# A fused three-layer kernel: MLP openings with products side by side, earlier first scores, a later output split, two banks for half blocks

## The reference

```python
# layer 0: banded attention (16 heads of 64, 4 KV heads, band of 3 blocks of 128 keys, sinks) + memory attention
# layer 1: two RG-LRU scans (forward, backward) with conv and gate + memory attention
for l in range(2):
    h = rms_norm(x, mix_norm[l])
    mixed, mq = attn_mixer(h, ...) if l == 0 else lru_mixer(h, ...)
    mo = memory_attention(mq, mk, mv)            # 4 heads of 128, 256 memory keys
    x = x + concatenate([mixed, mo]) @ w_out[l]
    x = x + square(relu(rms_norm(x, mlp_norm[l]) @ w_up[l])) @ w_down[l]   # 4096 hidden
x = rms_norm(x, final_norm)
# layer 2: stick-breaking attention + sliding window with sinks, gated; modulation from c_2 @ w_ada_2
```

## Time and profile before

| what | value |
|---|---|
| median of 3 runs | 3047.69 us (3042.49 to 3051.21) |
| the profiled execution | 3045.61 us, its span 3043.8 us |
| PE / DVE / ACT / POOL busy | 97% / 70% / 41% / 3% of the span |
| granted TensorE clock, mean | 0.992 |
| DMA | 190 MB, 63 GB/s over the span |
| chain that ended last | PE 80%, DVE 10%, ACT 7%, issue 2% |

### The profile page before, as it was taken

One profiled execution on the slowest core, in us unless ns is written; L12 is line 12 of the kernel. 1 busy time (PEld: TensorE's weight loads), 2 busy tenths in 40 slices (PEclk: granted clock), 3 DMA queues, 4 the chain that ended last, 5 costly groups with the idle time before them and its releaser, 6 DMA issues.

```text
span 3043.8 us, 35198 instructions
## 1 busy us (share of the span) xinstructions
PE 2956.6 (97%) x13896; PEld 2311.9 (76%) x13896; DVE 2142.7 (70%) x3303; ACT 1243.6 (41%) x2121; POOL 89.9 (3%) x70
## 2 busy tenths in 40 slices
PE   8999989999999999999999999999999999999998
PEld 7885557878888888888877788888888786666666
DVE  7746866687777777689964887777777735566675
ACT  4214642432222222478832522222223516876652
POOL 0003520000000000000000000000000000000000
PEclk9999999999999999999999999999999999999999
DMA  4430024111111111211131011111111131000213
GB/s 155 118 94 8 1 98 140 55 50 51 52 56 49 49 56 56 101 45 46 52 139 42 21 56 56 53 46 56 56 50 61 49 126 34 21 21 22 97 52 114
DMA packets 72804, 190.47 MB, mean 63 GB/s; under 512 B 8320, under 2 KB 8704, under 8 KB 72512
## 3 DMA queue, kind: packets, MB, share of 16 engines
q1 hardware_dynamic: 72640, 188.23, 19.2%
HBM read 172.20 MB, written 14.68 MB: 61 GB/s over the span
## 4 chain that ended last, share of the span: by engine, by line
PE 80%; DVE 10%; ACT 7%; issue 2%; DMA 0%; POOL 0%; SPq 0%; DVEq 0%; ACTq 0%; POOLq 0%
PE PS L1490 42%; PE PS L279 25%; PE PS L366 2%; DVE sm L908 2%; PE PS L320 1%; ACT p L926 1%; PE PS L887 1%; PE PS L873 1%; PE PS L2784 1%; PE PS L2801 1%; PE PS L899 1%; PE PS L2775 1%; PE PS L1092 1%; PE PS L1084 1%; ACT p L233 1%
## 5 line engine op out<-in xcount | busy, mean ns | idle before, releaser
L1490 PE MATMUL PS<-p 128*128 128x512 f32 x5760 | 1318.0, 391 | 13.3 <-DVE p L1401 7.7
L1490 PEld LDWEIGHTS PS<-p 128*128 128x128 f32 x5760 | 1083.0, 188 | 246.6 <-ACT p L1395 8.5
L279 PE MATMUL PS<-p 128*128 128x512 f32 (+1 forms) x4560 | 1057.0, 390 | 26.3 <-DVE p L475 9.6
L279 PEld LDWEIGHTS PS<-p 128*128 128x128 f32 x4560 | 840.5, 189 | 231.5 <-issue 39.8
L1687 DVE TENSOR_TENSOR p<-p,PS 128x512 f32<-128x512 f32 x480 | 327.7, 683 | 64.5 <-PE PS L1490 51.2
L241 DVE TENSOR_TENSOR p<-p 128x1024 fp32r<-128x1024 f32 x138 | 163.7, 1190 | 142.5 <-ACT p L233 142.3
L1299 DVE TENSOR_TENSOR p<-p 128x512 fp32r<-128x512 f32 x224 | 154.2, 688 | 112.3 <-ACT p L1293 111.4
L1627 ACT ACTIVATE p<-p 128x512 fp32r<-128x512 f32 x128 | 80.2, 628 | 346.0 <-DVE p L1676 329.6
L1293 ACT ACTIVATE p<-p 128x512 fp32r<-128x512 f32 x224 | 140.1, 625 | 184.9 <-PE PS L1490 159.5
L233 ACT ACTIVATE p<-p 128x1024 fp32r<-128x1024 f32 x138 | 141.7, 1030 | 172.9 <-PE PS L279 111.5
L926 ACT ACTIVATE p<-PS,sm 128x256 f32<-128x256 f32 (+2 forms) x256 | 127.9, 508 | 173.7 <-DVE sm L914 94.1
(11 more groups left out here) (236 smaller groups left out, 2785.3 us busy)
## 6 DMA issues: line engine op xcount, KB each, us to landing
p<-in_in_dram SPq DMA_DIRECT2D x72, 512.0 KB, 3.5
p<-in_up_dram SPq DMA_DIRECT2D x128, 256.0 KB, 2.6
p<-in_dn_dram SPq DMA_DIRECT2D x128, 256.0 KB, 2.6
p<-in_out_dram SPq DMA_DIRECT2D x42, 512.0 KB, 3.6
p<-in_ada_dram SPq DMA_DIRECT2D x24, 512.0 KB, 3.6
p<-in_x_dram SPq DMA_DIRECT2D x16, 512.0 KB, 8.0
p<-in_kv_dram SPq DMA_DIRECT2D x16, 512.0 KB, 3.5
spill_dram<-p SPq DMA_DIRECT2D x16, 512.0 KB, 3.9
```

Of the source, the lines that this page charges most:

```text
L279: ins = e.matmul(ps[:, c:c + m], weights(b, j, wi), x[:, c:c + m], start=first and i == 0, stop=end and i == 2)
L1490: ins = e.matmul(PS[:, bank, :], w[:, wi, :], x[:, xi, :], start=start and i == 0, stop=stop and i == 2, skip_group_check=open_)
```

## The change

1. **First scores.** The score halves 0 and 1 of the banded attention are issued after mq0 2, ahead of mq0 3. DVE scales mq0 3 (`dve_last_queries`) between the stats of halves 1 and 2, ACT's exponentials of unit 1 wait for that. `END0` is gone.
2. **Output split behind the copies.** ACT's L1018 comes after its copies L952; DVE's L1047 (`out_low`) moves into the next unit, between the stats and the normalisation of j=0.
3. **Boundary to memory attention 0.** Memory scores 0 and 1 are issued in units 32 and 33 of the banded loop, before its last transposes and values; DVE and ACT do their stats and exponentials of unit 0 there. PE, DVE no longer wait for `END1`, ACT waits for the last values only; SP's loads of X still wait for `END1`.
4. **Half blocks in two banks.** Fills 0 and 2 use bank 6, the others bank 7, in both memory stages. In memory attention 0 the fills of units 7 and 8 move between values and transposes, that of unit 9 ahead of the values. The modulation products follow the first tile of the projection, in bank 6.
5. **Memory attention 1.** ACT and DVE do `y_half(0)` before the block split; DVE scales the queries before the block split.
6. **MLP openings (both).** PE does product 0, then k = 0 to 2 of products 1, 2, 3, then their k = 3, then the total, then products 4, 5, (1,0), 6, (1,1) to (1,5). Products (1,0) and (1,3) use bank 5, which the first down product also uses; it now waits for ("t11", l, 1). Ring part 3 moves ahead of the last inputs; ring 7 goes before 6; 9 to 12, S4 and the root's halves are interleaved anew, the root and `dve_t("11")` of pair 0 come later, `dve_t("11")` of pair 1 before the first addition.

```diff
@@ pe_values0
-            pe_project(P, e, "in0", 4, 8, Hk("x0"), ("mq0",), lambda n: [("mq0t", n)])
+            P.pair = 1
+            pe_project(P, e, "in0", 3, 8, Hk("x0"), ("mq0",), lambda n: [("mq0t", n)])
+            for hs in range(2):
+                n, kp, half, kbs = UNITS0[0]
+                pe_window_scores(P, e, "b0", hs, hs, score_view(hs, 128 * len(kbs), True), n, kp, half, kbs, Qt, Kt, 4, bias0,
+                                 [*(("rotated", x) for x in range(10)), P.held[2 * hs], P.held[2 * hs + 1], ("cb",)])
+            P.pair = 2
+            pe_project(P, e, "in0", 1, 8, Hk("x0"), ("mq0", 3), lambda n: [("mq0t", 3)])
@@ dve_banded0
+                    if hs == 2:
+                        dve_last_queries(V, e)
...
+                    if j == 0 and u >= 3 and UNITS0[u - 3][2] == 1:
+                        out_low(u - 3)
                     if 1 <= hs <= 64:
...
@@ pe_banded0
+                    if j == 0 and u >= 32:
+                        for b in range(2):
+                            P.held[2 * (u - 32) + b] = [("exp", "b0", 30 + u)]
+                        pe_mem_scores(P, e, "m0", u - 32, MQ, MK, [("mq0t", 3), *(("mk0", n) for n in range(4))])
@@ pe_mem0
-                if FILLS[u] > 1:
+                if FILLS[u] > 1 or u == 9:
                     fill()
                 if u >= 2:
                     pe_mem_values(P, e, "m0", u - 2, MV, PTM0, None)
+                if u in (7, 8):
+                    fill()
...
-            pe_mod(P, e)
             P.pair = 0
-            pe_project(P, e, "out0", 8, 4, MOk(MO0, "m0"), ("xo", 0), lambda n: [("xb", 0, n)])
+            pe_project(P, e, "out0", 8, 4, MOk(MO0, "m0"), ("xo", 0), lambda n: [("xb", 0, n)], first=lambda: pe_mod(P, e))
@@
+        def fill_bank(i):
+            return 6 if i in (0, 2) else 7
+        def bank_of(j, o):
+            return 5 if j == 1 and o in (0, 3) else BANK[o]
@@ pe_mlp
-            for o in range(3):
-                pe_product(P, e, l, 0, o)
+            pe_product(P, e, l, 0, 0)
+            for o in (1, 2, 3):
+                pe_product(P, e, l, 0, o, 0, 3)
+            for o in (1, 2, 3):
+                pe_product(P, e, l, 0, o, 3, 4)
             pe_total(P, e, ("x", l), SQX[0], SQX[1][7], X_SUMMED[l], p=3, more=SQX[1][6])
-            for o in range(3, 7):
-                pe_product(P, e, l, 0, o)
-            for o in range(6):
-                pe_product(P, e, l, 1, o)
+            for j, o in ((0, 4), (0, 5), (1, 0), (0, 6), (1, 1), (1, 2), (1, 3), (1, 4), (1, 5)):
+                pe_product(P, e, l, j, o)
+            P.held[5] = [("t11", l, 1)]
@@ dve_first_pairs
+            dve_s3(V, e, l, 0)
+            ring(7)
             ring(6)
-            dve_s3(V, e, l, 0)
             dve_t(V, e, l, 0, "21")
-            ring(7)
             dve_t(V, e, l, 0, "22")
-            dve_root(V, e, ("x", l), *ROOTX)
-            dve_t(V, e, l, 0, "11")
             ring(8)
...
             ring(13)
+            dve_t(V, e, l, 1, "11")
             add(0, 0)
-            dve_t(V, e, l, 1, "11")
@@ act_mem1, dve_mem1
+                if u == 0:
+                    y_half(0)
                 if u < 2:
                     fill()
-                if u == 0:
-                    y_half(0)
```

More of the change, by code:

```diff
@@ L839, in dve_values0 @@
             e.tensor_scalar(vec[:, NV0:NV0 + 24], C("sinks", 0, 24), -1.0, None, ALU.mult).then_inc(*V.did(("nsinks",)))
-            for n in range(4):
+            for n in range(3):
                 block_lo(V, e)
@@ L844, in dve_values0, with dve_last_queries @@
                 e.tensor_tensor(MQ[:, n, :], got(("mq0", n)), R0, ALU.mult).then_inc(*V.did(("mq0t", n)))
-        END0 = [("mq0", 3), ("whi", 33), ("mq0t", 3), ("clear",)]
+            block_lo(V, e)
+        def dve_last_queries(V, e):
+            for s in V.need(("mq0", 3, 0)):
+                e.wait_ge(*s)
+            e.tensor_tensor(MQ[:, 3, :], got(("mq0", 3, 0)), R0, ALU.mult).then_inc(*V.did(("mq0t", 3)))
         def score_view(hs, nk, full):
@@ L1021, in act_banded0, with out_low @@
                             act_copy(A, e, "b0", u - 1, kb, PT0, TB0, pt_free[kb])
+                    if j == 1 and u >= 2 and UNITS0[u - 2][2] == 1:
+                        src, hh, hl = out0_of(u - 2)
+                        for s in A.need(("pv", "b0", u - 2)):
+                            e.wait_ge(*s)
+                        e.activation(hh, src, ACT.Copy).then_inc(*A.did(("oh", "b0", u - 2)))
         def dve_banded0(V, e):
-            for s in V.need(*END0):
-                e.wait_ge(*s)
             pt_free = [None] * 3
+            def out_low(u):
+                src, hh, hl = out0_of(u)
+                for s in V.need(("oh", "b0", u)):
+                    e.wait_ge(*s)
+                e.tensor_tensor(hl, src, fz(hh), ALU.subtract).then_inc(*V.did(("ol", "b0", u)))
             for u in range(34):
@@ L1132, in pe_mem0 @@
         def pe_mem0(P, e):
-            for s in P.need(*END1):
-                e.wait_ge(*s)
             fills = [(n, hf) for n in range(8) for hf in range(2)]
@@ L1186, in dve_mem0 @@
         def dve_mem0(V, e):
-            for s in V.need(*END1):
-                e.wait_ge(*s)
             dve_cond(V, e)
@@ L1212, in dve_mem0 @@
                     dve_ada(V, e, 3 * u - 2)
-                fill()
+                if u < 7:
+                    fill()
                 if 1 <= u <= 8:
@@ L1609, in act_first_sum @@
                 e.wait_ge(*s)
-            e.activation(quota(j, "12"), PS[:, 0, :], ACT.Copy).then_inc(*A.did(("s1", l, j)))
+            e.activation(quota(j, "12"), PS[:, bank_of(j, 0), :], ACT.Copy).then_inc(*A.did(("s1", l, j)))
         SPOT = {"11": (0, 0), "21": (0, 1), "12": (1, 0), "22": (1, 1)}
@@ L1776, in dve_first_pairs @@
                 dve_made(V, e, l, 1, name)
+            dve_root(V, e, ("x", l), *ROOTX, only=0)
+            ring(9)
+            dve_root(V, e, ("x", l), *ROOTX, only=1)
+            ring(10)
+            dve_made(V, e, l, 1, "S4")
+            ring(11)
+            dve_t(V, e, l, 0, "11")
             dve_q(V, e, l, 0, "11")
             dve_r(V, e, l, 0, "21")
-            ring(9)
             dve_t(V, e, l, 0, "12")
@@ L1789, in dve_first_pairs @@
             dve_r(V, e, l, 0, "12")
-            ring(11)
             dve_down(V, e, l, 0, 1)
```

127 lines of the change are left out of this document (63 added, 64 removed).

## The result

| | before | after |
|---|---|---|
| median | 3048.03 us (4 runs, 3042.49 to 3051.21) | 3016.39 us (4 runs, 3014.92 to 3021.25) |
| ratio after/before, 95% interval | | 0.990, 0.9884 to 0.9917 |
| profiled execution, its span | 3045.6, 3043.8 us | 3016.5, 3014.7 us |
| granted TensorE clock, mean | 0.992 | 0.994 |

The change takes 31.6 us off the median and 29.1 us off the profiled span: 1%, and the interval leaves out 1. 3021 had been predicted, in 3008 to 3034.

The account below looks back on a forecast made before the run. PE, busy 2956.6 of 3043.8 us, was taken as the bound, leaving only its idle and low-clock time to win. Gains 5.8 + 3.7 + 3.5 + 2.4 + 9.2 + 1.8 = 26.4 us off 3047.7 gave 3021, range 3008 to 3034.

Parts of the forecast that it names:

- three small waits: Banded attention start: PE waits 0.3 us for bank 4, 0.9 for the normalisation, 0.4 for the copy out of bank 4.
- The first rival: Start of the banded attention stays at the lower clock: 5.8 us gain becomes 2.5, 3024.6 us; chance 0.15.
- The pair: Two banded units, one with an output: 11.66 us before, forecast to gain 0.31 us.
- number of places: Banded attention, output split: 0.31 us gained per pair of units, counted over 12 pairs, 3.7 us.
- what comes back: Banded pairs: 0.57 of the 0.88 us saved was to return as a wait on POOL's later scaling.
- The waits: Memory attention 0: second fill's 0.83 us and normalisation waits of 0.47 and 1.52 us shrink; gain 0.8 + 1.6.
- The modulation products cost the same where they stand now: Memory attention 0, first projection tile: moving these products was to bring no gain, nothing counted.
- The new wait: MLP openings, before the first down product: PE waits 5.7 and 6.4 us for bank 5, the kernel's longest.
- bank 5 is free in time: Rival, MLP openings: part of DVE's chain overlaps, up to 16.9 us more gain, 3004 us; chance 0.08.
- bank 5 comes later still: Rival, MLP openings: DVE waits for an unseen ACT copy or DMA, some 4 us each, 3030 us; chance 0.10.

Follow-up runs that it names:

- e6: Changed kernel with no scores ahead of the last query block, the banded attention starting as in the kernel before: 3021.12 us.
- e1: Changed kernel with the output split ahead of the copies again on ACT and DVE: 3016.99 us.
- e7: Changed kernel with DVE's low half of the output behind the normalisation again: 3017.4 us.
- e5: Changed kernel with DVE's evacuation of t11 of pair 1 moved up to behind the first down split: 3005.62 us.
- e2: Changed kernel with both MLP openings as they were before the change: 3022.23 us.
- e3: Changed kernel with memory attention 1's half blocks in bank 7 alone, the changed order kept: 3022.97 us.
- e4: Changed kernel with the down products' bank rotation moved on by one: 3007.1 us.
- e8: e5 with all 16 additions behind the evacuation moved up among the first down blocks too: 3003.35 us.
- e9: The changed kernel as it is, timed again: 3014.97 us (4 runs), ratio to the kernel before 0.990.
- e10: e8 without further edit, timed again beside the changed kernel: 3001.16 us (4 runs), ratio to the kernel before 0.9854.
- e12: e8 with the modulation columns in six groups of four between products of the first two output tiles: 3002.74 us (5 runs), ratio 0.9856.

## Why the prediction was right

**1. First scores, 5.8 forecast, 6.9 measured, 6.9 by e6.** The mechanism and the three small waits were right; unit 4 began 58.3 us behind the first query, against 59.4 by the forecast. The first rival, a clock that stays low, did not happen: 1.00 from 245 us on. On the rule that transposes don't count as activity (the Trainium skill, TensorE: Matmul & The Clock Gate, Part 4: PE-mode transpose) the trace shows no such effect: the stretch from 245 to 255 us, made of short scores and transposes, ran at 1.00. The kernel issues them with `e.transpose` against an identity, and the rows show them as MATMUL; whether that is the page's mode, and what transposes without other products between them would do, no run here shows.

**2. Output split, 3.7 forecast, 5.06 measured (e1).** The pair, 11.35 forecast, took 11.38. Mis-sized was the number of places: 12 full pairs give 3.4, and the rest of the stretch gave 1.7 that I had not counted. And one detail was wrong: not all of what comes back is POOL's. 0.31 us are, and 0.20 us are bank 7's release by L1043. e7 shows that the two trade: with the low half behind the normalisation POOL's waits fall to 0.7 us in all, and those for bank 7 rise to 12.5.

**3. Boundary, 3.5 forecast, 3.6 by subtraction.** The gain of the stretch without part 2 is 7.0 - 5.06 = 1.9, and with the second memory score of 1.7 us, which it now contains, 3.6. No run takes this part back alone.

**4. Two banks and fills, 2.4 forecast, 1.7 measured in the profiled execution.** The waits went as forecast: 2.8 us of them became 0.25. Against that stands the clock behind the modulation products, low for 10.2 us in after (548.0 to 558.2) and for 6.8 in before (559.0 to 565.8), and half of the difference, 1.7 us, was lost by that. It is not the change's own. The profiles that have the changed code from the first fill to the first product of MLP 0 differ in it:

| clock low behind the products | that stretch | profiles |
|---|---|---|
| 3.4 us | 170.0 us | e7 |
| 6.8 us | 171.6 us | e1, e5 |
| 10.2 us | 173.2 us | after, e2, e3, e4, e6, e8, e9, e10 |

With 6.8 us of low clock, as in before, the part gains 3.3 us, 0.9 more than forecast; that much I did not take apart. "The modulation products cost the same where they stand now" can't be told closer than these 3.2 us, and no run takes this part back alone.

**5. Memory attention 1, 9.2 forecast, 9.6 measured.** e3 splits it: 5.6 by the bank, 4.0 left for the order.

**6. MLP openings, 1.8 forecast, 3.5 measured; by e2, 2.4.** The new wait stood where it was forecast, on bank 5, released by the evacuation of t11: 5.99 and 5.68 us, where 5.7 and 6.4 were worked out. DVE's list up to it took 46.7 us in both openings, against 47.25 and 47.6. The clock cost 1.7 and 2.5 us, against 2.4 each. Of the rivals, neither *bank 5 is free in time* nor *bank 5 comes later still* came about; the first was had by e8, at 3001 us where it was priced at 3004.

On idle gaps (the Trainium skill, TensorE: Matmul & The Clock Gate, Why this matters for your kernels) these runs agree for the long ones: behind the waits of 5.99 and 5.68 us the clock was at 0.50. But shorter ones brought it down too, and the length alone does not decide. The clock went to 0.50 for 3.4 us at waits of 3.08 and 3.26 us (e4) and 2.31 us (e5, MLP 1), and stayed at 1.00 at 2.15 us (e5, MLP 0). In the kernel before it stayed at 1.00 behind 1.82 us (MLP 0) and fell for 3.4 us behind 1.85 us (MLP 1), at the same place of the same code.

**What the forecast did not see** is that the wait of part 6 was worth removing and cheap to remove. I had taken DVE as the bound, since it is busy 44 of 50 us. e5 and e8 show that it was not: the same DVE work in another order lets PE run on for 49.75 us without a gap, 14 us off the time. So the 5.99 and 5.68 us were forecast rightly for the order as written, but what I held against the rival *bank 5 is free in time*, that DVE is nearly full, was no reason.

The remaining difference, 31.6 us of the medians against 26.4, is the 3.9 us of the table (30.3 against 26.4), less 1.2 (start and end), plus 2.5 of spread between executions: the profiled one of before was 2.4 us faster than its median. That half is chance.

## What to carry to other kernels

When an in-order engine is nearly full, ask of each wait on it whether the operation waited for could stand earlier; busy 95% says that the engine's list is long, not that the order in it is right. Moving one 0.68 us operation up by 7 us of work (e5) took 9.5 us off the two MLPs, and the whole rearrangement of PE's products 2.4 (e2). And price a low clock together with the wait: where the next input is only just in time, taking the low clock away yields a wait (e12).

## What the runs showed of the hardware

- A run of 48 one-column products, in which PE is recorded busy without a gap, is followed by a low clock in every one of the 13 profiles that have it: 3.4 to 10.2 us at 0.50. In six groups of eight between full products the clock stays at 1.00 (e12). A full busy share in the rows is thus no sign that the clock stays up.
- The same code behind those products took 170.0, 171.6 or 173.2 us in different executions, by how long the clock stayed low: 3.4, 6.8 or 10.2 us.
- The releaser in a bracket can be a neighbour: for L911 in after it names L951, while e7 shows that L1043 is what frees the bank.
- The first query stood at 196.6 to 197.6 us in seven profiles and at 199.8 to 200.3 in the other seven, with the same code before it. All have a wait of 2.1 us near 90 us; the late ones are just those in which the clock fell to 0.50 for 3.4 us behind it, which costs 1.7; their first 96 products also took 24.6 to 24.9 us instead of 23.4 to 23.8. Totals of single executions can't tell parts of 3 us; stretches between marks of PE's own work could, to some 0.1 us where the clock was the same.
